# A transformer block pair on one core: first-half input projection and convolution made inside the expert stage, pooling on GpSimd, mask rows in attention

## The chip, the cores and the metric

The kernel runs on one core of a Trainium2 chip, in float32 throughout. The metric is the device time of one execution in microseconds (us), lower is better. The core has five instruction streams: TensorE (PE: matmuls; PEld: its weight loads), VectorE (DVE), ScalarE (ACT), GpSimd (POOL) and SyncE (SP, which here only issues weight loads). They share an on-chip memory (SBUF), 128 partitions wide; matmuls write into PSUM banks. Every dependence between engines is a semaphore wait written by hand, so an engine stands still at a wait even where later instructions could run.

## The reference

```python
def first_block(x, ...):
    h = rms_norm(x, g_mix[l]);  p = h @ w_in[l]
    y_a = mla_group(p[..., :MLA_COLS], ...)          # 8 heads, chunk-causal attention
    y_b = rwkv7_group(p[..., MLA_COLS:], ...)        # recurrent branch
    x = x + jnp.concatenate([y_a, y_b], -1) @ w_o[l]
    x = x + peer_ffn(rms_norm(x, g_ffn[l]), ...)     # 128 experts per token, rows gathered
    return x

def peer_ffn(...):   # per token: 8 heads x top 16
    u = expert_u[idx]; act = gelu(einsum('thkd,td->thk', u, hb)); vv = expert_v[idx]
    return einsum('thk,thkd->td', gate * act, vv)

def second_block(x, c, ...):
    h = layer_norm(x) * (1.0 + sc1) + sh1
    proj = h @ w_in[l]                               # 3584 columns
    a_val, a_gate, u_pool, gate_a, gate_b = split(proj)
    ya = a_val * sigmoid(a_gate)
    ya = causal_dwconv(ya, w_dw_a[l], b_dw_a[l])     # 31 taps, 512 channels
    ya = silu(layer_norm(ya, ...)) @ w_pw_a[l]
    yb = einsum(causal_multiscale_pool(u_pool), w_pool[l]) * pool_scale[l]   # windows 2, 4, 8, 16
    merged = sigmoid(gate_a) * ya + sigmoid(gate_b) * yb
    x = layer_norm(ALPHA * x + g1 * (merged @ w_out[l]), ...)
    ...                                              # gated FFN with 3 taps, 2 x 2816 columns
    return x
```

There are 512 tokens, 1024 channels; a query in a 64-token chunk sees that chunk and all before it.

## The kernel before

The 512 tokens are four tiles of 128 (`NT` = 4, t = 0 to 3; "tiles one and two" are t = 0, 1, tokens 0 to 255). The stages run one after another: the first block's projections, attention (32 units: tile x head), the recurrent branch, the output projection, the expert stage, and then the second block: input projection, convolution and pooling, `w_out`, the FFN.

**Channels.** PE hands results to ACT over four PSUM banks "a" (PA) and to DVE over four banks "d" (PD). Results are numbered; the table `JOBS` gives the first number of each stage on either channel, and ACT or DVE takes them strictly in order. A bank is reused once result j-3 was taken.

**Weights.** SP loads weight chunks of mostly 2048 KB in one fixed order into slots (mostly the three slots of `WR`). A load waits until the last use of the chunk that held the slot (L484), and all later loads wait behind it.

**Attention.** In unit u PE writes a score tile (L590), adds the mask to its last 128 columns by a second matmul of one row (L592: `lowrow` times `negrow`), transposes the probabilities of unit u-1 and multiplies those of u-2 with the values. Between units stand eight of the fourteen projections of the recurrent branch (`projection(m)`, eight matmuls of 512 columns each; `PR_EARLY` = 4 are made before, in front of the transposes of q and k). ACT copies each into `RAW`, and DVE mixes it with its token before (`mix(m)`, L1416 and L1417).

**Expert stage.** For each tile 128 steps k. POOL gathers one expert row per token, 1 MB for 128 tokens, into one of eight ring buffers (L1981), DVE forms the dot product (L1838), ACT makes the gate and a diagonal matrix of it (L1202, L1204, L1208), PE adds diagonal times row into two banks (L882) and so frees the buffer for the gather eight steps on. In tile t DVE also selects the experts of tile t+1. In tile 0 PE makes query projections between the steps (L859, 128 matmuls of 256 columns, ACT copies each result of eight).

**Second block's input projection.** Behind the last step, PE makes 28 blocks of 128 columns (seven chunks of `w_in2`, eight matmuls a block, all 512 tokens), the first four in two parts (L902, then L908 for the last tile). Chunk order: gate of the convolution, its value (the one that goes to DVE), pooling input, gates a, gates b. DVE multiplies value by gate (L1854), convolves 4 x 31 taps over 512 tokens (L1858, L1860), normalizes by two column sums that PE makes with a matrix of ones (4 matmuls each, placed in the last chunk), and then pools (L1894 to L1905). PE follows with the pooling product and the pointwise product (`yb`, `pw`), DVE merges (L1910 to L1916), then `w_out`.

## Time and profile before

| | |
|---|---|
| median of three runs | 2820.36 us (2818.66 to 2823.57) |
| the profiled execution | 2828.96 us, of which its span 2827.4 us |
| mean granted TensorE clock | 0.963 of full speed |
| PE busy | 2412.7 us (85%) |
| DVE busy | 1522.6 us (54%) |
| ACT busy | 704.7 us (25%) |
| POOL busy | 537.1 us (19%) |
| gathers by POOL | 512, 536.90 MB |

Times in the views count from the span's start. A float32 matmul is recorded twice on PE, so x64 there is 32 matmuls. A row's second number is busy time from the first start to the last end; for what one of several back-to-back instructions costs, take the distance of starts. "[7.29 <-issue]" is idle time ahead of the row and what ended it.

### The profile page before, as it was taken

To read this page: it belongs to the slowest core of one execution; us is meant where nothing else is said; L and a number is where in the kernel's file an instruction comes from. 1 tells how busy PE (TensorE), PEld (TensorE's weight loads), DVE (VectorE), ACT (ScalarE), POOL (GpSimd) and SP (SyncE) were. 2 spreads that over 40 slices of the span, in tenths; PEclk is the share of its full clock that TensorE was granted. 3 is DMA by queue.
4 is the path that set the end of the run, shared out by engine and by line. 5 is a ranking of instruction groups with operands and counts; after the bars stand their busy time and mean duration, and the time that the engine had idled before them with its cause. 6 is when DMAs were issued, how large, how long until landed. Compare 5 with 4: busy or idle time off the path is not lost.

```text
span 2827.4 us, 27190 instructions
## 1 busy us (share of the span) xinstructions
PE 2412.7 (85%) x9764; PEld 1184.4 (42%) x9764; DVE 1522.6 (54%) x3250; ACT 704.7 (25%) x2064; POOL 537.1 (19%) x516
## 2 busy tenths in 40 slices
PE   6889888798898977777777777788899898999998
PEld 3455478666444432222222222222354343444443
DVE  3555367638566646666576655554348464333204
ACT  1122221110333334333433343333200101111000
POOL 0000000000444534434343433333100000000000
PEclk9989869899999999999999999999999999999999
DMA  3301440311999999999999999999521312212110
GB/s 131 111 1 60 147 152 10 126 70 47 422 418 419 421 414 421 421 421 420 416 418 416 417 417 419 421 421 416 215 72 55 134 41 79 89 60 89 65 69 30
DMA packets 130102, 663.71 MB, mean 235 GB/s; under 512 B 9520, under 2 KB 12208, under 8 KB 64048
## 3 DMA queue, kind: packets, MB, share of 16 engines
q0 software_dynamic: 73728, 536.90, 45.8%
q1 hardware_dynamic: 56240, 125.08, 12.3%
q8 instruction: 77, 1.26, 0.2%
q14 instruction: 57, 0.47, 0.0%
HBM read 659.85 MB, written 2.10 MB: 234 GB/s over the span
## 4 chain that ended last, share of the span: by engine, by line
PE 53%; DMA 28%; DVE 8%; issue 6%; ACT 4%; PEld 1%; PEldq 0%; POOL 0%; SPq 0%; DVEq 0%; another core or an unknown queue 0%; ACTq 0%; POOLq 0%
DMA AR<-in_uv,C 27%; PE PA L525 22%; PE PD L882 10%; PE PD L525 8%; PE PA L859 2%; PE PD L954 1%; PE PA L954 1%; ACT C L1208 1%; PE PD L693 1%; PE PD L518 1%; PE PA L693 1%; DVE AR L1838 1%; ACT SC L1204 1%; PE PA L755 1%; PE PA L902 1%
## 5 line engine op out<-in xcount | busy, mean ns | idle before, releaser
L882 PE MATMUL PD<-AR,C 128*128 128x512 f32 x2048 | 1001.2, 614 | 262.2 <-ACT C L1208 261.2
L1838 DVE CUSTOM_DVE_ANT_0 AR<-AR,HN 128x1024 f32<-128x1024 f32 x512 | 626.3, 1224 | 509.9 <-DMA AR<-in_uv,C 506.9
L1981 POOL DMA_INDIRECT AR<-in_uv,C x512 | 536.9, 1049 | 1471.3 <-PE PD L882 740.8
L882 PEld LDWEIGHTS PD<-AR,C 128*128 128x128 f32 x2048 | 356.1, 190 | 842.1 <-ACT C L1208 567.9
L525 PE MATMUL PA<-AR,WR 128*128 128x512 f32 (+1 forms) x720 | 313.0, 603 | 4.7 <-ACT AR L1091 3.2
L1202 ACT ACTIVATE SC<-SC 128x1 f32<-128x1 f32 x512 | 103.7, 203 | 684.2 <-DVE SC L1838 683.8
L525 PE MATMUL PA<-HT,WR 128*128 128x512 f32 (+1 forms) x736 | 260.9, 515 | 0.0
L525 PEld LDWEIGHTS PA<-AR,WR 128*128 128x128 f32 (+1 forms) x720 | 138.1, 193 | 179.3 <-issue 176.4
L1208 ACT ACTIVATE C<-C,SC 128x128 f32<-128x128 f32 x512 | 205.5, 401 | 16.8
L525 PEld LDWEIGHTS PA<-HT,WR 128*128 128x128 f32 x736 | 125.6, 193 | 127.6 <-issue 127.6
L1204 ACT ACTIVATE SC<-SC,C 128x1 f32<-128x1 f32 x512 | 150.8, 294 | 16.6
L1949 DVE TENSOR_SCALAR HT<-HN,V 128x512 f32<-128x512 f32 x44 | 24.0, 546 | 197.1 <-ACT HN L1242 197.1
L525 PE MATMUL PD<-WR,HT 128*128 128x512 f32 (+1 forms) x320 | 120.0, 534 | 3.1 <-DVE HT L1916 1.6
L1242 ACT COPY HN<-PA 128x512 f32<-128x512 f32 x44 | 25.8, 586 | 267.8 <-PE PA L525 267.8
L1860 DVE SCALAR_TENSOR_TENSOR AR<-AR,V 128x512 f32<-128x512 f32 x120 | 90.2, 752 | 4.3
L954 PE MATMUL PD<-WR,AR 128*128 128x512 f32 x176 | 86.9, 610 | 5.3 <-DMA WR<-in_w_down 5.3
L954 PE MATMUL PA<-WR,AR 128*128 128x512 f32 x176 | 84.2, 593 | 1.4 <-ACT HN L1242 0.9
L525 PEld LDWEIGHTS PD<-WR,HT 128*128 128x128 f32 x320 | 57.0, 190 | 63.1 <-issue 58.8
L1014 ACT ACTIVATE SC<-SC 128x1 f32<-128x1 f32 (+4 forms) x33 | 6.8, 207 | 264.6 <-DVE SC L1278 261.3
L859 PE MATMUL PA<-HT,WR 128*128 128x256 f32 x256 | 72.1, 379 | 0.0
L859 PEld LDWEIGHTS PA<-HT,WR 128*128 128x128 f32 x256 | 48.9, 191 | 51.1 <-issue 49.8
L1960 DVE TENSOR_TENSOR HN<-PD,RW 128x512 f32<-128x512 f32 x4 | 2.8, 692 | 98.3 <-PE PD L954 98.3
(372 smaller groups left out, 2180.8 us busy)
## 6 DMA issues: line engine op xcount, KB each, us to landing
WR<-in_w_ada SPq DMA_DIRECT2D x12, 2048.0 KB, 9.5
WR<-in_w_in SPq DMA_DIRECT2D x11, 2048.0 KB, 7.9
WR<-in_w_up SPq DMA_DIRECT2D x11, 2048.0 KB, 7.9
WR<-in_w_down SPq DMA_DIRECT2D x5, 2048.0 KB, 7.9
WR<-in_w_pq SPq DMA_DIRECT2D x4, 2048.0 KB, 17.7
AR<-in_uv,C POOLq DMA_INDIRECT x512, 15.3
AR<-in_w_pq SPq DMA_DIRECT2D x3, 2048.0 KB, 12.9
WR<-in_w_o SPq DMA_DIRECT2D x2, 2048.0 KB, 8.3
```

The costliest lines, as they stand in the source:

```text
L518: ins = nc.tensor.transpose(b[0:cols, rows * i:rows * i + rows], src, ident[0:rows, 0:rows])
L525: ins = nc.tensor.matmul(b, lhsT, rhs, start=(i == 0), stop=(i == len(pairs) - 1))
L693: ins = nc.tensor.matmul(b[at:at + 64, 64 * i:64 * i + 64], lhsT, rhs, start=True, stop=True)
L859: ins = nc.tensor.matmul(b_pq[0][:, 0:2 * P], wq[:, k, P * (m % 4):P * (m % 4) + P], HT[:, k, 2 * P:S], start=(k == 0), stop=(k == KD - 1))
L882: ins = nc.tensor.matmul(acc[half], DG[:, j, :], UV[:, j, D + 512 * half:D + 512 * half + 512], start=(k == 0), stop=(k == NSEL - 1))
L954: ins = nc.tensor.matmul(banks[half][t], FT[:, k, P * t:P * t + P], w[:, kk, 512 * half:512 * half + 512], start=(k == 0), stop=(k == NF - 1))
L1202: tell(A(GEL[:, j:j + 1], DOT[:, j:j + 1], ACT.Gelu), "gelu")
L1204: tell(A(GEL[:, j:j + 1], GEL[:, j:j + 1], ACT.Copy, scale=GATE[:, t % 2, k:k + 1]), "gated")
L1208: tell(A(DG[:, j, :], ident, ACT.Copy, scale=GEL[:, j:j + 1]), "diag")
L1838: ttr(UV[:, j, 0:D], UV[:, j, 0:D], HN[:, t, :], 1.0, 0.0, ALU.mult, ALU.add, DOT[:, j:j + 1]).then_inc(s["dots"], 1)
L1860: link(stt(CV[:, m, :], YAP[:, m, j:j + 512], w[:, j:j + 1], CV[:, m, :], ALU.mult, ALU.add))
L1981: nc.gpsimd.indirect_dma_start(UV[:, ring_slot(turn), :], None, uv, bass.IndirectOffsetOnAxis(ap=IDX[:, t % 2, i:i + 1], axis=0),).then_in ...
```

## The change

It has four parts. (1) **Half in the expert stage.** All 28 blocks of the input projection are made for tokens 0 to 255 in the expert stage, one matmul of 256 columns a step, from step 32 of tile t = 2 on (96 steps there, 128 in t = 3); the chunks of `w_in2` are loaded once for it and a second time for tokens 256 to 511. ACT copies each block into free SBUF (with one Sigmoid for the gate after block 3). DVE multiplies value by gate at steps 100 to 103 of t = 2 and does the 124 taps of the first half, one a step, from step 112 on. The later input projection and convolution are then 256 tokens wide; ACT moves the parts made early to their places. (2) **Pooling** goes from DVE to GpSimd. (3) **Mask rows.** Four rows under q and k hold the mask, so the scores need one matmul; GpSimd writes them in 16 instructions as soon as the constants are there. (4) Two more projections of the recurrent branch stand ahead of the transposes of q and k (`PR_EARLY` = 6, three more `RAW` buffers), and two fewer between the units; DVE mixes two of them before unit 0.

```diff
+HALF_FROM, MUL_AT, CONV_FROM = 32, 100, 112
+def half_step_at(t, k):
+    if t == 2 and k >= HALF_FROM:
+        return k - HALF_FROM
+    return k + P - HALF_FROM if t == 3 else None
+def conv_step_at(t, k):
+    c = k - CONV_FROM if t == 2 else k + P - CONV_FROM if t == 3 else -1
+    return c if 0 <= c < 4 * CONV_K else None
...
-PR_EARLY, PR_IN_ATT = 4, 12
+PR_EARLY, PR_IN_ATT = 6, 12
...
-    put("lowrow", (j < 64) & (i == 0))
-    put("negrow", np.where((j >= 64) & (i == 0), np.float32(-1e30), np.float32(0)))
+    put("lowrow", j < 64)
+    put("negrow", np.where(j >= 64, np.float32(-1e30), np.float32(0)))
...
+        for q, i in enumerate(in2_order):
+            col_chunk(w_in2, 512 * i, 512, "a", half_job(4 * q + 3))
         for i, (ch, j) in zip(in2_order, in2_last):
             col_chunk(w_in2, 512 * i, 512, ch, (FIRST_A if ch == "a" else FIRST_D)["in2"] + j)
...
                 if i == CNUM["wout"]:
                     sp.wait_ge(s["row2free"], 1)
+                    sp.wait_ge(s["moved"], 4)
+                    sp.wait_ge(s["pooled"], 4)
                     sp.dma_start(R2, row2).then_inc(s["in_row2"], 16)
...
-                    nc.tensor.matmul(b[:, 0:nk], QKT[0:DQK, h, P * t:P * t + P], QKT[0:DQK, H + h, 0:nk],
-                                     start=True, stop=False)
-                    full("a", nc.tensor.matmul(b[:, nk - P:nk], cc("lowrow")[0:1, :], cc("negrow")[0:1, :],
-                                               start=False, stop=True))
+                    full("a", nc.tensor.matmul(b[:, 0:nk], QKT[0:DQK + NT, h, P * t:P * t + P],
+                                               QKT[0:DQK + NT, H + h, 0:nk], start=True, stop=True))
...
+            def half_step(c):
+                m, k = c // KD, c % KD
+                w = chunk(pe, CNUM["in2a"] + m // 4)
...
+                ins = nc.tensor.matmul(b_half[0][:, 0:2 * P], w[:, k, P * (m % 4):P * (m % 4) + P], HT[:, k, 0:2 * P],
+                                       start=(k == 0), stop=(k == KD - 1))
...
             for i in range(1, 7):
                 w = chunk(pe, CNUM["in2"] + i)
-                if i == 6:
-                    pe.wait_ge(s["conv"], 4)
-                    product("d", [(cc("ones"), CV[:, m, :]) for m in range(4)])
                 for m in range(4):
-                    if i == 6 and m == 2:
-                        pe.wait_ge(s["convsq"], 4)
-                        product("d", [(cc("ones"), HN[:, q, 0:512]) for q in range(4)])
+                    if i == 6 and m == 1:
+                        pe.wait_ge(s["conv"], 4)
+                        product("d", [(cc("ones"), CV[:, q, :]) for q in range(4)])
                     product("d" if i == 1 else "a",
-                            [(w[:, k, P * m:P * m + P], HT[:, k, :]) for k in range(KD)])
+                            [(w[:, k, P * m:P * m + P], HT[:, k, 2 * P:S]) for k in range(KD)], 2 * P)
+            pe.wait_ge(s["convsq"], 4)
+            product("d", [(cc("ones"), HN[:, q, 0:512]) for q in range(4)])
...
+                    c = half_step_at(t, k)
+                    if c is not None and c % KD == KD - 1:
+                        half_copy(c // KD)
...
+                    c = conv_step_at(t, k)
+                    if c is not None:
+                        j_, m = divmod(c, 4)
...
+                            ins = stt(CV1[:, m, :], YAP1[:, m, j_:j_ + 2 * P], w[:, j_:j_ + 1], CV1[:, m, :],
+                                      ALU.mult, ALU.add)
...
+            pool.wait_ge(s["in_const"], 64)
+            which = ident[DQK:DQK + NT, DQK:DQK + NT].unsqueeze(2).broadcast_to([NT, NT, P])
+            for g in range(2 * H):
+                row = cc("lowrow" if g < H else "negrow")[DQK:DQK + NT, :].unsqueeze(1).broadcast_to([NT, NT, P])
+                nc.gpsimd.tensor_tensor(QKT[DQK:DQK + NT, g, :].rearrange("p (t n) -> p t n", t=NT), which, row,
+                                        ALU.mult).then_inc(s["masked"], 1)
...
+            pool.wait_ge(s["a_free"], FIRST_A["in2"] + 8)
+            pool.wait_ge(s["d_free"], FIRST_D["in2"] + 4)
+            pool.wait_ge(s["moved"], 2)
+            pool.wait_ge(s["bufs"], 1)
+            for m, w in enumerate(POOL):
...
```

PE at the end of the expert stage, before: the last steps of two accumulating matmuls each (L882; x96 is 48 steps), the input projection (L902 to L525), with the two ones products (the x4 rows, which wait for DVE) inside its last blocks, then the pooling and pointwise products (x40) and `w_out`.

```order
L882 MATMUL PD<-AR,C 128x512 x96
L902 MATMUL PA<-HT,WR 128x384 x32
L518 MATMUL PD<-C,HN 128x128 x8
L908 MATMUL PA<-HT,WR 128x128 x32
L525 MATMUL PD<-HT,WR 128x512 x32
L525 MATMUL PA<-HT,WR 128x512 x128
L525 MATMUL PD<-AR,C 128x512 x4
L525 MATMUL PA<-HT,WR 128x512 x16
L525 MATMUL PD<-HN,C 128x512 x4
L525 MATMUL PA<-HT,WR 128x512 x16
L525 MATMUL PD<-AR,WR 128x512 x40
L525 MATMUL PD<-WR,HT 128x512 x32
```

PE at the same place after the change (L909 is the early half, L932 the step of the expert stage):

```order
L909 MATMUL PA<-HT,WR 128x256
L932 MATMUL PD<-AR,C 128x512 x2
L909 MATMUL PA<-HT,WR 128x256
L954 MATMUL PA<-HT,WR 128x128 x32
L554 MATMUL PD<-C,HN 128x128 x8
L960 MATMUL PA<-HT,WR 128x128 x32
L561 MATMUL PD<-HT,WR 128x256 x32
L561 MATMUL PA<-HT,WR 128x256 x136
L561 MATMUL PD<-AR,C 128x512 x4
L561 MATMUL PA<-HT,WR 128x256 x24
L561 MATMUL PD<-HN,C 128x512 x4
L561 MATMUL PD<-AR,WR 128x512 x40
```

A matmul of 256 columns now stands between the steps, the projection behind them has half the columns, the first ones product (`PD<-AR,C ... x4`) stands ahead of the last three blocks, and the second behind them.

GpSimd after the change; before it had the 512 gathers (the DMA row) alone. Rows up to the first windows of the pooling:

```order
L2048 TENSOR_TENSOR AR<-C 4x512 x16
L2061 DMA AR<-in_uv,C 128x2048 x512
L2086 TENSOR_TENSOR AR<-AR 128x512
L2091 TENSOR_TENSOR AR<-AR,C 128x16
L2092 TENSOR_SCALAR AR<-AR 128x496
L2093 TENSOR_TENSOR AR<-AR 128x512
L2085 MEMSET AR 128x16
L2086 TENSOR_TENSOR AR<-AR 128x512 x2
```

The 16 mask instructions stand at the front and the pooling at the end; L2086 to L2093 ahead of the MEMSET are the first of four windows, and each larger one has one addition (with a MEMSET) more.

PE at the start of attention, before (the first two rows are the last transposes of q and k, L590 and L592 scores and mask):

```order
L518 MATMUL PA<-C,AR 96x128 x4
L518 MATMUL PD<-C,AR 96x128 x4
L590 MATMUL PA<-AR 128x128
L592 MATMUL PA<-C 128x128
L590 MATMUL PA<-AR 128x128
L592 MATMUL PA<-C 128x128
L518 MATMUL PD<-C,AR 128x128
```

and after:

```order
L554 MATMUL PA<-C,AR 96x128 x4
L554 MATMUL PD<-C,AR 96x128 x4
L627 MATMUL PA<-AR 128x128 x2
L554 MATMUL PD<-C,AR 128x128
L627 MATMUL PA<-AR 128x128
L554 MATMUL PD<-C,AR 128x128
L561 MATMUL PD<-AR 128x64
```

One matmul a unit is gone.

## Rows read from the trace of the kernel before

**Rows 1.** The page: DMA's GB/s in 40 equal slices; median time to landing

```profile
GB/s 131 111 1 60 147 152 10 126 70 47 422 418 419 421 414 421 421 421 420 416 418 416 417 417 419 421 421 416 215 72 55 134 41 79 89 60 89 65 69 30
...
AR<-in_uv,C POOLq DMA_INDIRECT x512, 15.3
```

**Rows 2.** Windows: busy time of each engine, granted clock, DMA share, GB/s

```profile
713.00:2029.00 1316.00, 1057.11 (x2401) 418.00 (x2402) 800.87 (x1775) 496.43 (x1626) 529.22 (x504) 1.00 1.00 414
2029.00:2279.00 250.00, 238.83 (x617) 113.53 (x616) 142.54 (x215) 24.46 (x35) 0.00 (x0) 0.98 0.21 74
```

**Rows 3.** DMA queues in 980:1060, where three chunks of w_in2 land (packets, MB, share)

```profile
q1 hardware_dynamic: 3120, 6.29, 20.8%
```

**Rows 4.** Windows of the expert stage, tile 0, with query projections on PE

```profile
880.00:940.00 60.00, 54.58 (x153) 28.30 (x152) 40.90 (x91) 22.84 (x80) 27.40 (x23) 1.00 1.01 421
```

**Rows 5.** Timeline of PE, expert stage, tile 0 (start us, us)

```profile
906.27 1.88 PE L882 MATMUL PD<-AR,C 128*128 128x512 f32 x4
907.99 0.59 PE L859 MATMUL PA<-HT,WR 128*128 128x256 f32 x2
908.42 1.88 PE L882 MATMUL PD<-AR,C 128*128 128x512 f32 x4
```

**Rows 6.** Timeline of DVE and POOL, expert stage

```profile
1079.72 1.22 DVE L1838 CUSTOM_DVE_ANT_0 AR<-AR,HN 128x1024 f32<-128x1024 f32 x1 [1.25 <-DMA AR<-in_uv,C]
1079.82 1.94 POOL L1981 DMA_INDIRECT AR<-in_uv,C  x1 [2.08 <-PE PD L882]
1082.06 0.93 POOL L1981 DMA_INDIRECT AR<-in_uv,C  x1 [0.31 <-issue]
```

**Rows 7.** Timeline of PE from the expert stage's end to w_out

```profile
2028.62 20.88 PE L902 MATMUL PA<-HT,WR 128*128 128x384 f32 x64 [0.47 <-issue]
...
2052.67 9.04 PE L908 MATMUL PA<-HT,WR 128*128 128x128 f32 x64 [2.30 <-DVE HT L1845]
2061.55 27.63 PE L525 MATMUL PD<-HT,WR 128*128 128x512 f32 x64
...
2202.31 13.90 PE L525 MATMUL PA<-HT,WR 128*128 128x512 f32 x32
...
2240.66 36.54 PE L525 MATMUL PD<-AR,WR 128*128 128x512 f32 x80 [7.29 <-issue]
2278.78 27.73 PE L525 MATMUL PD<-WR,HT 128*128 128x512 f32 x64 [1.58 <-DVE HT L1916]
```

**Rows 8.** Timeline of DVE in the same stretch and at w_out

```profile
2163.56 23.59 DVE L1860 SCALAR_TENSOR_TENSOR AR<-AR,V 128x512 f32<-128x512 f32 x30
...
2219.68 0.69 DVE L1875 TENSOR_SCALAR HN<-PD 128x512 f32<-128x512 f32 x1 [12.15 <-PE PD L525]
...
2224.51 2.50 DVE L1880 TENSOR_TENSOR AR<-AR,HN 128x512 f32<-128x512 f32 x4
...
2245.55 5.04 DVE L1910 SCALAR_TENSOR_TENSOR HT<-PD,V,AR 128x512 f32<-128x512 f32 x6 [0.26 <-PE PD L525]
...
2340.26 1.28 DVE L1770 SCALAR_TENSOR_TENSOR X<-X,SC,AR 128x1024 f32<-128x1024 f32 x1
```

**Rows 9.** Timeline of PE, attention

```profile
150.21 1.09 PE L518 MATMUL PA<-C,AR 128*96 128x128 f32 x4 [18.11 <-DVE AR L1407]
...
237.79 0.48 PE L592 MATMUL PA<-C 1*128 1x128 f32 x2
238.20 0.55 PE L518 MATMUL PD<-C,AR 128*128 128x128 f32 x3
```

**Rows 10.** Timeline of DVE, start of attention

```profile
161.79 0.29 DVE L1429 TENSOR_REDUCE SC<-PA 128x1 f32<-128x128 f32 x1 [1.01 <-PE PA L592]
...
162.90 0.75 DVE L1417 SCALAR_TENSOR_TENSOR AR<-AR,V 128x512 f32<-128x512 f32 x1
```

**Rows 11.** Start: timeline of DVE, and time to landing of the last constant

```profile
14.26 0.16 DVE L1282 TENSOR_TENSOR SC<-SC 128x4 f32<-128x4 f32 x1
...
SC<-in_pos SPq DMA_DIRECT2D x1, 2.0 KB, 9.6
```

More of the change, by code:

```diff
@@ L254, in build @@
                  "topk", "idx", "dots", "geluv", "gates", "gelu", "gated", "diag", "uv_used", "csil", "rowdiag",
-                 "bufs", "conv", "convsq", "silu_in", "silu", "pooled", "merged",
+                 "bufs", "siga", "yam", "moved", "pooling", "conv", "convsq", "silu_in", "silu", "pooled", "merged",
                  "lnx", "upraw_used", "gelu_in", "ff", "fin", "row2free",
@@ L315, in build @@
         GF = C[:, CONST["lowrow"][0]:CONST["lowrow"][0] + D]
-        ROWDIAG = HN[:, 0:2, :].rearrange("p a b -> p (a b)")
+        ROWDIAG = CAND
+        YAP1 = ar(18432, 4 * 286, 4)
+        SGA1 = ar(19576, 1024, 4)
+        CV1 = SGA1
+        GA1 = ar(20600, 2048, 8)
+        UP1 = HN[:, 0, :].rearrange("p (a b) -> p a b", a=4)
+        GB1 = [HN[:, 1, :].rearrange("p (a b) -> p a b", a=4), HN[:, 2, :].rearrange("p (a b) -> p a b", a=4)]
         def y0(k):
@@ L862, in query_step @@
                     full("a", ins)
+            b_half = [None]
+            def half_step(c):
+                m, k = c // KD, c % KD
+                w = chunk(pe, CNUM["in2a"] + m // 4)
+                if c == 0:
+                    pe.wait_ge(s["a_free"], half_job(0))
+                if k == 0:
+                    b_half[0] = bank("a")
+                ins = nc.tensor.matmul(b_half[0][:, 0:2 * P], w[:, k, P * (m % 4):P * (m % 4) + P], HT[:, k, 0:2 * P],
+                                       start=(k == 0), stop=(k == KD - 1))
+                if k == KD - 1:
+                    full("a", ins)
             for j in range(16):
@@ L887, in _ @@
                         ins.then_inc(s["uv_used"], 1)
+                    if half_step_at(t, k) is not None:
+                        half_step(half_step_at(t, k))
                     if t == 0:
@@ L901, in _ @@
                 for k in range(KD):
-                    nc.tensor.matmul(first[m][:, 0:S - P], w[:, k, P * m:P * m + P], HT[:, k, 0:S - P],
+                    nc.tensor.matmul(first[m][:, 0:P], w[:, k, P * m:P * m + P], HT[:, k, 2 * P:3 * P],
                                      start=(k == 0), stop=(k == KD - 1))
@@ L907, in _ @@
                 for k in range(KD):
-                    ins = nc.tensor.matmul(first[m][:, S - P:S], w[:, k, P * m:P * m + P], HT[:, k, S - P:S],
+                    ins = nc.tensor.matmul(first[m][:, P:2 * P], w[:, k, P * m:P * m + P], HT[:, k, S - P:S],
                                            start=(k == 0), stop=(k == KD - 1))
@@ L1054, in _ @@
                 raw(t)
+            for m in range(NT, PR_EARLY):
+                raw(m)
             for g in range(0, 2 * H, 2):
@@ L1183, in turned_both, with half_copy @@
                     turned_block(HT, t, k0, lambda k: modc[:, 8 + k:9 + k], lambda k: modc[:, k:k + 1])
+            def half_copy(b):
+                q, m = divmod(b, 4)
+                dst = (SGA1[:, m, :], YAP1[:, m, 30:286], UP1[:, m, :], GA1[:, m, :], GA1[:, 4 + m, :],
+                       GB1[0][:, m, :], GB1[1][:, m, :])[q]
+                tell(nc.scalar.copy(dst, take()[:, 0:2 * P]), "a_free")
+                if b == 3:
+                    act.wait_ge(s["a_free"], half_job(3) + 1)
+                    tell(A(SGA1, SGA1, ACT.Sigmoid), "siga")
             gate_exp(0)
@@ L1418, in mix @@
                 tell(dve.nop(), "prt")
+            for m in range(2):
+                mix(m)
             units = [(t, h) for t in range(NT) for h in range(H)]
@@ L1442, in _ @@
                     link(ts(HN[:, t, 64 * h:64 * h + 64], b[:, 0:64], st_a[:, 32:33], None, ALU.mult), "d_free")
-                if u < PR_EARLY:
-                    mix(u)
+                if u + 2 < PR_EARLY:
+                    mix(u + 2)
                 if pr_after(u - 2) is not None:
@@ L1984, in _, with joined @@
                     ).then_inc(uv_full[ring_slot(turn)], 16)
+            def joined(ins, name="pooling"):
+                tell(ins, name)
+                pool.wait_ge(s[name], n[name])
+            tt_, ts_ = nc.gpsimd.tensor_tensor, nc.gpsimd.tensor_scalar
+            pool.wait_ge(s["a_free"], FIRST_A["in2"] + 8)
[3 more added lines that the diff above has]
+            for m, w in enumerate(POOL):
+                u = UP[:, m, :]
+                src = u
+                step = 1
+                bufs_ = [ar(16600, 528), ar(17128, 528)]
+                i = 0
+                while step < w:
+                    dst = bufs_[i % 2]
+                    if 2 * step < w:
+                        joined(nc.gpsimd.memset(dst[:, 0:16], 0.0))
+                    joined(tt_(dst[:, 16:528], src[:, 16:528], src[:, 16 - step:528 - step], ALU.add))
+                    src = dst
+                    step *= 2
+                    i += 1
+                cn_ = cc("cnt")[:, 16 * m:16 * m + 16]
+                joined(tt_(src[:, 16:32], src[:, 16:32], cn_, ALU.mult))
+                joined(ts_(src[:, 32:528], src[:, 32:528], 1.0 / w, None, ALU.mult))
+                joined(tt_(PO[:, m, :], src[:, 16:528], u[:, 16:528], ALU.subtract), "pooled")
 def kernel(**inputs):
```

101 lines of the change are left out of this document (55 added, 46 removed).

## The prediction

> **What bounds the kernel now.** I read the page first: from slice 11 to 28 DMA moves 414 to 422 GB/s [rows 1]. The table of windows says what that stretch is: over the 1316 us of the expert stage DMA is busy with share 1.00, while PE has 1057 us, DVE 801 and ACT 496 [rows 2]. So the gathers set the pace, about 2.49 us for each 1.048 MB at 421 GB/s, and every other engine has room; what is put into this stage is free on PE, DVE and ACT and costs full price on DMA. The 250 us behind it are the opposite: DMA share 0.21, PE busy 238.8 of 250 [rows 2], and the timeline of PE shows matmuls almost end to end from 2028.62 to the start of `w_out` at 2278.78, 250.2 us [rows 7]. In attention the timeline of PE has no idle entry in the units shown, but 18.11 us of idle before the transposes of q and k [rows 9].
>
> **End of the expert stage to `w_out`, the large gain.** I time it from E, 2028.62 [rows 7].
> - PE. The first four blocks are now twice 32 matmuls of 128 columns, 9.0 us each by L908; between them lie the transposes and DVE's eight small copies, which took from 2049.5 (2028.62 + 20.88) to 2052.67, 3.2 us [rows 7]. That is E+21.3. A matmul of 256 columns takes 0.43 us (907.99 to 908.42 [rows 5]), a block of eight 3.45; of 512 columns a block took 6.9 (27.63 for four [rows 7]). The four value blocks end at E+35.1, the sixteen next and one of the last chunk at E+94, where PE now waits for the convolution.
> - DVE. Its last multiplication ends at E+35.6. A tap on 512 columns takes 0.786 us (23.59 for 30 [rows 8]). 256 columns are in no row: such an instruction on 1024 columns takes 1.28 and on 512 it takes 0.75 [rows 8, 10], so 256 less columns save 0.265 and a tap is 0.52. Four rows of 30 taps and a cheaper first one are 16.0 each, 64.2 together: the convolution ends at C = E+100 if nothing disturbs DVE.
> - From C to `w_out`: ones product 3.5, three blocks 10.4, ones product 3.5, so C+17.4 (DVE's centring and squares, four instructions each like the 2.50 of L1880 [rows 8], hide in it). From there before's rows give the rest: 2219.68 to 2227.01, 7.3, for variance, root, reciprocal and scaling [rows 8]: C+24.7. Then `yb` leaves DVE every 0.84 us (5.04 for six [rows 8]); PE needs five of them gone before the pointwise product gets its first bank, 4.3, then eight products of 3.43, 27.4, and 1.6 for the merge [rows 7]: `w_out` starts at C+58. That is E+158, 92 us earlier than before.
> - Pooling on GpSimd. It starts when the pooling input of tiles three and four is copied, about E+50, right inside the convolution. Its 28 instructions (14 two-input ones of 512 columns, 4 of 496 with one input, 4 of 16, 6 memsets) have no row. DVE takes about 0.63 for such a two-input one (2.50 for the four of L1880), GpSimd's own gather instruction 0.93 to 1.94 [rows 6, 8]. I take 1.1, near the unhindered one, and 0.7 for one input: 19 us in all. GpSimd's own time is hidden: the result is due at C+17. Its neighbour is not: at 1079.82 a gather instruction began 0.10 us after a dot product of DVE and took 1.94 instead of 0.93, that is until the dot product's end and then its usual time [rows 6]. So a GpSimd instruction is kept out while DVE reads two SBUF tensors. Whether DVE is kept out in turn, no row shows: the price lies between nothing and GpSimd's whole 19 us. A tap reads two SBUF tensors, and I take the whole: C = E+119.
>
> The Trainium skill (SBUF — State Buffer, "SBUF: two separate sides") says that the port pair is an exclusive lock for a whole instruction between a GpSimd instruction and a DVE one with two SBUF inputs; by that rule the sum is the one with 19 us, without it the one of the rival below, and the row at 1079.82 agrees for one direction. The GPSIMD Engine Reference, section 3, gives 4497 ns for a two-input addition of 2048 columns, which makes an estimate of 1.1 us for 512.
>
> PE then idles from E+94 to E+119. Before, after 18.11 us of idle, four transposes took 1.09 us where later three take 0.55 [rows 9], about the ratio of TensorE's two levels, 1.2 and 2.4 GHz; a first ones product at the lower one costs 3.4 more. Together `w_out` starts at E+180.5: **-69.7 us**.
>
> **Loads, the price.** The seven chunks are loaded for the early half, and of the second set two more come before E; before, three came there (2048 KB each). Six more loads compete with the gathers: 12.6 MB at 421 GB/s are 29.9 us. By the share of DMA time it is more: 6.29 MB took 20.8% of 80 us, 5.5 a load [rows 3], 33.3 for six. I take **+32**. The step on PE grows from 1.72 to 2.15 us (906.27 to 908.42, where tile 0 had just this mix [rows 5]), below 2.49. ACT waits for PE in each block, some 2 us every eight steps; a gather takes 15.3 us from issue to landing where 2.5 is its share [rows 1], so this much delay empties nothing, and tile 0 had the same at 421 GB/s [rows 4]. DVE's tap adds 0.5 to 1.3 us. The later chunks load while PE works on two others, and the row vectors behind `pooled` have C-dependent work of 58 us in front: both free. If that cover went, a chunk costs its 8 to 10 us.
>
> **Attention.** Two projections of 6.9 us move into 18.11 us of idle [rows 9]: -13.8. 32 mask matmuls at 0.41 (237.79 to 238.20 [rows 9]): -13.1. Against it: DVE mixes two projections before unit 0, 1.4 each (0.75 and about as much [rows 10]), of which 1.01 was idle: +1.9. In the small units of tiles 0 and 1 PE may now wait for the exponentials, between 0 and the whole 0.41 of 16 units, 6.6; I take +3. With 14 us less idle ahead of the transposes the clock may stay at its upper level in them (1.09 for four now, against 0.55 for three later): 0 to 6 us, taken as -2. **-24**, from -19 to -29.
>
> **The start.** GpSimd's 16 mask instructions run from the landing of the constants (the last 9.6 us after its issue at about 4.1, so 13.7 [rows 11]), 17.6 us at 1.1. From 14.26 on DVE makes the rows that PE transposes and the angles; I count ten instructions with two SBUF inputs until 21.3, linked one by one, and PE's first projection waits for what follows them. By the same hold, ten times 1.1: **+11**, bounds 0 and 17.6.
>
> Sum: 11 - 24 + 32 - 69.7 = -50.7. The profiled execution (2828.96, span 2827.4 and 1.6 around it) would be 2778.3; it stood 8.6 above the median, so against 2820.36 I say **2769**.
>
> **Rivals.**
> 1. DVE is not held by GpSimd. Then start 0, C = E+100, PE idles 6 us only: -24 + 32 - 92 = -84, 2736. For it: no DVE row is stretched beside a gather. Against: those hold SBUF for a moment at most, and the hold in the other direction is visible. Chance 0.25.
> 2. GpSimd is slower than I think. At 1.94 us, the dearest of its rows, the pooling holds DVE 33 us instead of 19 and the start costs up to 19 instead of 11: 2769 + 14 + 8 = 2791; up to 2814 if its instructions take 3 us or `wout` loads then come late (they stand behind `pooled` on SP). Chance 0.16.
> 3. Slower than before: ACT's in-order wait for each early block isn't absorbed. ACT stands 2 to 2.7 us in each of 28 blocks; if the gathers felt it, 28 x 2.7 = 76 us, and 76 - 50.7 = +25, 2845. It turns slower at 1.9 us a block. Against it stands tile 0, with 16 such blocks at full GB/s [rows 4]. Chance 0.05.
> 4. The early half brings nothing because the end is bound elsewhere, and loads eat attention's gain: about 2815 to 2825. Against it are PE's 238.8 of 250 us. Chance 0.03.
> My forecast, 2755 to 2785, has 0.51.
>
> **How the numbers follow.** A measurement tells 0.2% (5.6 us) from no change. Rival 3 is slower, rival 4 mostly the same, the rest faster: 0.92, 0.03, 0.05. The range reaches from rival 1 with 6 us for the unknown clock and attention terms to rival 2's 2791 with 5: 2730 to 2796.
>
> **What would show it.** Right: expert stage about 32 us longer at 415 to 421 GB/s; convolution taps 0.49 busy, with some 19 us of gaps or stretched ones while GpSimd pools; PE idle before the first late ones product; `w_out` 180 us behind the last step; scores without L592's successor and an idle before the transposes of 4 us. Wrong: DVE rows of usual length beside GpSimd's (then 2736), a GpSimd instruction near 2 us, DMA share under 0.95 in t = 2 and 3, or the transposes of q and k starting late because ACT copies six projections.

## The result, and the profile after

The changed kernel takes 2774.74 us (median of 4 runs, 2770.58 to 2776.05) beside 2819.51 for the kernel before on the same chip (now the median of 4; with 3 it was 2820.36): ratio 0.9829, 95% interval 0.9813 to 0.9845, so 1.7% less, well clear of the noise. Its profiled span is 2768.5 us.

The kernel before was profiled a second time later (`e9_before_again`, span 2817.4, its time 2819.0 is nearer the median than that of the profile shown ahead). The stages, cut at PE's first product, the first transpose of q and k, the first product of the modulation, the load of `keys` just ahead of the first expert step, the first late projection (E) and `w_out`:

| stage | before | before again | after | forecast |
|---|---|---|---|---|
| start to first product | 24.7 | 24.8 | 36.0 | +11 |
| to the transposes of q and k | 125.6 | 125.6 | 127.1 | 0 |
| attention | 150.2 | 150.3 | 137.8 | -24 |
| modulation and recurrence | 411.2 | 398.7 | 393.9 | 0 |
| expert stage | 1316.9 | 1319.5 | 1354.9 | +32 |
| E to `w_out` | 250.2 | 250.1 | 170.6 | -69.7 |
| rest | 548.6 | 548.5 | 548.2 | 0 |

Against the second profile the sum is 48.9 us less. Every stage for which a change was forecast moved to that side, but three have another size than forecast: attention gave half, the end stage 10 more, and the first profile alone would credit 17 us to a stage that the change doesn't touch.

**Start.** DVE and GpSimd, timeline (start us, us; in brackets the idle time ahead and who ended it); this answers to [rows 11]:

```profile
14.11 0.52 DVE L1355 TENSOR_TENSOR SC<-SC 128x4 f32<-128x4 f32 x1
14.66 0.97 DVE L1356 SCALAR_TENSOR_TENSOR SC<-SC 128x4 f32<-128x4 f32 x1
...
16.67 5.84 DVE L1387 TENSOR_SCALAR HN<-X,SC 128x1024 f32<-128x1024 f32 x4
22.43 1.01 DVE L1403 CAST SC<-SC 128x4 f32<-128x4 int32 x1
...
29.53 0.94 DVE L1413 TENSOR_SCALAR SC<-SC 128x64 f32<-128x64 f32 x1
30.50 0.97 DVE L1414 TENSOR_SCALAR SC<-SC 128x64 f32<-128x64 f32 x1
31.50 0.19 DVE L1415 TENSOR_SCALAR SC<-SC 128x64 f32<-128x64 f32 x1
```

```profile
13.57 17.84 POOL L2048 TENSOR_TENSOR AR<-C 4x512 f32<-4x512 f32 x16 [13.14 <-DMA SC<-in_pos]
```

Look where the length of DVE's rows changes: from 22.43 on 0.94 to 1.02 us each until 31.50, 0.19 from there on, and GpSimd's row ends at 31.41. TENSOR_SCALAR and CAST, which have one tensor from SBUF, are held as long as those with two. PE's first product, behind 6.76 us of idle, then begins at the lower clock (0.50 granted in 36 to 38 us, where it was 1.00 before) and takes 29.13 us in place of 27.70; this is the 1.5 us of the second stage.

**Stages.** Windows of the changed kernel (busy time of each engine, granted clock, DMA share, GB/s), answering to [rows 2]:

```profile
163.10:300.90 137.80, 125.38 (x496) 78.03 (x496) 70.17 (x194) 35.94 (x112) 0.00 (x0) 0.87 0.09 31
300.90:694.80 393.90, 333.73 (x4617) 267.58 (x4616) 248.99 (x585) 75.63 (x153) 5.85 (x6) 0.90 0.28 101
694.80:2049.70 1354.90, 1136.73 (x2848) 511.04 (x2849) 851.75 (x1904) 507.50 (x1658) 558.02 (x506) 0.99 1.00 413
2049.70:2220.30 170.60, 143.62 (x616) 107.64 (x616) 107.93 (x187) 24.78 (x40) 25.41 (x28) 0.94 0.34 121
```

The expert stage still runs at DMA share 1.00 and 413 GB/s, with 80 us more of PE and 51 more of DVE inside. Attention has a granted clock of 0.87; before it was 0.95. PE's waits in attention (us in total, times, longest):

```profile
PE PD L554 <- ACT AR L1119: 8.8, 6, 4.7
PE PA L554 <- DVE AR L1481: 4.4, 1, 4.4
PE PD L554 <- DVE HN L1519: 2.3, 2, 1.7
PE PA L627 <- ACT AR L1109: 0.8, 1, 0.8
```

The idle of 18.11 us before the transposes [rows 9] is 4.4 now, as forecast; 12 us of waits inside the units stand beside it, where the kernel before had 4.7 (the window less PE's busy time).

**From E to `w_out`.** PE's timeline, answering to [rows 7]:

```profile
2081.32 58.87 PE L561 MATMUL PA<-HT,WR 128*128 128x256 f32 x272
...
2158.64 5.35 PE L561 MATMUL PD<-AR,C 128*128 128x512 f32 x8 [18.45 <-DVEq L1959]
2163.82 10.52 PE L561 MATMUL PA<-HT,WR 128*128 128x256 f32 x48
2174.18 3.60 PE L561 MATMUL PD<-HN,C 128*128 128x512 f32 x8
...
2220.30 27.73 PE L561 MATMUL PD<-WR,HT 128*128 128x512 f32 x64 [1.58 <-DVE HT L1990]
```

DVE's convolution beside it, answering to [rows 8], and some of GpSimd's pooling:

```profile
2082.06 0.41 DVE L1954 TENSOR_SCALAR AR<-AR,V 128x256 f32<-128x256 f32 x1
2082.51 16.46 DVE L1956 SCALAR_TENSOR_TENSOR AR<-AR,V 128x256 f32<-128x256 f32 x30
2099.14 1.38 DVE L1954 TENSOR_SCALAR AR<-AR,V 128x256 f32<-128x256 f32 x1 [0.18 <-DVE AR L1956]
2100.56 25.59 DVE L1956 SCALAR_TENSOR_TENSOR AR<-AR,V 128x256 f32<-128x256 f32 x30
2126.30 0.41 DVE L1954 TENSOR_SCALAR AR<-AR,V 128x256 f32<-128x256 f32 x1 [0.15 <-DVE AR L1956]
2126.75 15.59 DVE L1956 SCALAR_TENSOR_TENSOR AR<-AR,V 128x256 f32<-128x256 f32 x30
```

```profile
2095.80 1.11 POOL L2086 TENSOR_TENSOR AR<-AR 128x512 f32<-128x512 f32 x1 [66.64 <-ACT AR L1294]
...
2107.08 1.04 POOL L2086 TENSOR_TENSOR AR<-AR 128x512 f32<-128x512 f32 x1
...
2108.36 2.22 POOL L2086 TENSOR_TENSOR AR<-AR 128x512 f32<-128x512 f32 x2
2110.66 0.28 POOL L2091 TENSOR_TENSOR AR<-AR,C 128x16 f32<-128x16 f32 x1
2111.03 1.67 POOL L2092 TENSOR_SCALAR AR<-AR 128x496 f32<-128x496 f32 x1
...
2121.77 1.50 POOL L2093 TENSOR_TENSOR AR<-AR 128x512 f32<-128x512 f32 x1
```

GpSimd pools from 2095.80 to 2123.27. Thirty taps take 15.59 us without it, 25.59 beside it. The convolution is late for PE: 18.45 us of idle before the ones product. Single taps show that the hold comes and goes. The first of these begins beside a two-input addition of GpSimd (2107.08 above), the others beside its scaling of one input (2111.03):

```profile
2107.14 1.26 DVE L1956 SCALAR_TENSOR_TENSOR AR<-AR,V 128x256 f32<-128x256 f32 x1
...
2111.42 0.70 DVE L1956 SCALAR_TENSOR_TENSOR AR<-AR,V 128x256 f32<-128x256 f32 x1
...
2112.15 0.48 DVE L1956 SCALAR_TENSOR_TENSOR AR<-AR,V 128x256 f32<-128x256 f32 x1
```

The first tap ends at 2108.40, 0.28 us behind the addition's end at 2108.12; a tap alone takes 0.48. So it waited for the whole addition. This happens once for each of GpSimd's 14 two-input instructions of 512 columns: 13 taps take 1.14 to 1.38 us, and the TENSOR_SCALAR at 2099.14 takes 1.38 in place of 0.41, 11.0 us lost together. One tap beside each of the four scalings takes 0.70, 0.9 us lost together, and the taps between take their usual 0.48. In the other direction, GpSimd's two-input instructions take 1.04 us where no tap is in their way and up to 1.51 where one is under way.

### The profile page after: what moved, and what is told of

The parts are those of the page before. It is cut to its first block, busy times and chain, and to the rows that moved or that the text cites. A ratio compares the mean times of both kernels' runs of the same rounds, so it can differ in the third digit from the quotient of the medians.

```text
span 2768.5 us, 28188 instructions
## 1 busy us (share of the span) xinstructions
PE 2377.3 (86%) x10148; PEld 1260.4 (46%) x10148; DVE 1551.5 (56%) x3352; ACT 714.6 (26%) x2099; POOL 607.3 (22%) x560
## 4 chain that ended last, share of the span: by engine, by line
PE 48%; DMA 28%; DVE 12%; issue 6%; ACT 4%; PEld 1%; PEldq 0%; POOL 0%; SPq 0%; DVEq 0%; ACTq 0%
DMA AR<-in_uv,C 27%; PE PA L561 17%; PE PD L932 11%; PE PD L561 7%; DVE AR L1956 3%; PE PD L1005 1%; PE PA L894 1%; PE PA L1005 1%; DVE AR L1935 1%; ACT C L1271 1%; PE PD L554 1%; PE PD L728 1%; PE PA L728 1%; ACT SC L1267 1%; PE PA L554 1%
## 5 line engine op out<-in xcount | busy, mean ns | idle before, releaser
L932 PE MATMUL PD<-AR,C 128*128 128x512 f32 x2048 | 998.6, 612 | 214.7 <-ACT C L1271 210.6
L2061 POOL DMA_INDIRECT AR<-in_uv,C x512 | 563.9, 1101 | 1433.9 <-PE PD L932 750.2
L932 PEld LDWEIGHTS PD<-AR,C 128*128 128x128 f32 x2048 | 363.6, 191 | 675.0 <-ACT C L1271 402.7
L561 PE MATMUL PA<-HT,WR 128*128 128x256 f32 (+2 forms) x736 | 191.6, 422 | 0.0
L561 PEld LDWEIGHTS PA<-HT,WR 128*128 128x128 f32 x736 | 125.7, 192 | 60.3 <-issue 52.2
L909 PE MATMUL PA<-HT,WR 128*128 128x256 f32 x448 | 134.0, 381 | 2.9 <-ACT RW L1261 2.9
L909 PEld LDWEIGHTS PA<-HT,WR 128*128 128x128 f32 x448 | 85.6, 191 | 110.8 <-issue 110.8
L894 PE MATMUL PA<-HT,WR 128*128 128x256 f32 x256 | 72.6, 382 | 0.0
L894 PEld LDWEIGHTS PA<-HT,WR 128*128 128x128 f32 x256 | 49.1, 192 | 51.0 <-issue 49.7
L1956 DVE SCALAR_TENSOR_TENSOR AR<-AR,V 128x256 f32<-128x256 f32 x120 | 69.1, 576 | 4.3
## 6 DMA issues: line engine op xcount, KB each, us to landing
WR<-in_w_ada SPq DMA_DIRECT2D x12, 2048.0 KB, 11.3
```

Source lines behind the costliest of these rows:

```text
L561: ins = nc.tensor.matmul(b, lhsT, rhs, start=(i == 0), stop=(i == len(pairs) - 1))
L894: ins = nc.tensor.matmul(b_pq[0][:, 0:2 * P], wq[:, k, P * (m % 4):P * (m % 4) + P], HT[:, k, 2 * P:S], start=(k == 0), stop=(k == KD - 1))
L909: ins = nc.tensor.matmul(b_half[0][:, 0:2 * P], w[:, k, P * (m % 4):P * (m % 4) + P], HT[:, k, 0:2 * P], start=(k == 0), stop=(k == KD - 1))
L932: ins = nc.tensor.matmul(acc[half], DG[:, j, :], UV[:, j, D + 512 * half:D + 512 * half + 512], start=(k == 0), stop=(k == NSEL - 1))
L1956: link(stt(cv, YAP[:, m, 2 * P + j:S + j], w[:, j:j + 1], cv, ALU.mult, ALU.add))
L2061: nc.gpsimd.indirect_dma_start(UV[:, ring_slot(turn), :], None, uv, bass.IndirectOffsetOnAxis(ap=IDX[:, t % 2, i:i + 1], axis=0),).then_in ...
```

## The experiments

Every ratio is to the kernel before, timed beside it. The changed kernel has 0.9829 in its own comparison and 0.9819 in `e5_after_again`.

**e5_after_again and e10_after_third: the changed kernel again.**

> The changed kernel once more, as a control beside the three others of this call: 0.983 times the kernel before, about 2775.

2772.34 us, 0.9819 (0.9785 to 0.9853). The profile of e5 has the two stretches, attention and what follows, at other lengths than the first:

```profile
164.70:292.60 127.90, 115.35 (x496) 69.77 (x496) 69.58 (x195) 36.09 (x112) 0.00 (x0) 0.95 0.10 34
292.60:692.60 400.00, 338.15 (x4617) 269.01 (x4616) 248.97 (x585) 75.88 (x153) 6.80 (x7) 0.89 0.29 102
```

The same kernel, the same instructions (496 matmuls), 10 us less in attention at a clock of 0.95 where the first profile had 0.87.

> The changed kernel, profiled a third time, beside e9_before_again. Theory A: the same stretch takes 394 to 400 us, with 79 to 89 at the lower clock as in the first two profiles. Theory B: it can take 411 us too. Attention takes 128 or 138 us, according to 13 or 36 us at the lower clock.

Span 2771.8, one run of 2773.85 us; attention 137.8 at 0.87 and then 393.9 at 0.90, as in the first. This is what theory A says of the second stretch, but it doesn't refute B, which allowed 394 to 411; for the kernel before, the next run decides.

**e9_before_again: the kernel before again.**

> The kernel before, profiled a second time. Question: the stretch from the first product of the modulation to the load of the keys took 411.3 us before and 393.9 after, with 116 and 79 us of it at the lower clock, though the change touches nothing in it. Theory A (the clock's phases there belong to the kernel: how the work ahead of the stretch lies sets them): again about 411 us with 116 at the lower clock, and the time is 2820. Theory B (they vary from execution to execution, as attention did in the changed kernel, 137.8 and 127.9 us in two profiles): anywhere from 394 to 411 us, and the 17 us between the two first profiles are no part of what the change gives.

```profile
150.30:300.60 150.30, 145.60 (x592) 86.02 (x592) 69.76 (x195) 37.21 (x114) 0.00 (x0) 0.95 0.08 29
300.60:699.30 398.70, 336.93 (x4617) 270.00 (x4616) 248.80 (x585) 75.74 (x153) 5.78 (x6) 0.89 0.28 100
```

Theory B: 398.7 us this time, where the first profile took 411.2 at a clock of 0.86. So 12.5 of the 17 us lie between two profiles of one kernel and are no part of what the change gives. To compare such stretches I multiply the length by the granted clock, which gives about the length had PE, their bound, run at 2.4 GHz throughout (an estimate: the clock has two digits, so it is good to 1 us in attention and 2 in the other): 411.2 x 0.86 = 353.6 and 398.7 x 0.89 = 354.8 before, 393.9 x 0.90 = 354.5 and 400.0 x 0.89 = 356.0 after. Within that, the second stretch didn't change. Attention: 150.3 x 0.95 = 142.8 before, 137.8 x 0.87 = 119.9 and 127.9 x 0.95 = 121.5 after, some 22 less.

**e1_mask_late: the mask rows some 7 us later.**

```diff
             pool.wait_ge(s["in_const"], 64)
+            pool.wait_ge(s["sscan"], 2)
             which = ident[DQK:DQK + NT, DQK:DQK + NT]...
```

(`sscan` counts up when DVE's last two angle rows are done.)

> The changed kernel, with GpSimd's 16 mask instructions held back until DVE has made the angles of the rotary embedding (some 7 us later by the kernel before), so that they run while DVE reads PSUM. Theory (GpSimd holds every DVE instruction on SBUF beside it, also those with one input): DVE's small instructions take 0.19 us again where they took 0.97, HN's four scalings 2.7 us where they took 5.8, PE's first product starts 11 to 12 us sooner (24.7 us from the start of the span), and the time falls by 12 to about 2763. Rival 1 (something else is late, as the constants' landing): the start stays and the time is 2775. Rival 2 (the hold only moves): DVE's copies out of PSUM, 33 to 36 us in the changed kernel, are stretched in their turn and half of the gain is given back, 2769. A new phase of the granted clock behind the start can add or take up to 10 us in either case, so the start is judged by its rows.

2763.01 us, 0.9777 (0.9754 to 0.9800). DVE and GpSimd:

```profile
14.63 2.74 DVE L1387 TENSOR_SCALAR HN<-X,SC 128x1024 f32<-128x1024 f32 x4
...
19.21 0.20 DVE L1414 TENSOR_SCALAR SC<-SC 128x64 f32<-128x64 f32 x1
...
21.14 2.94 DVE L1377 TENSOR_SCALAR HT<-PD,V 128x512 f32<-128x512 f32 x4
```

```profile
21.25 16.07 POOL L2049 TENSOR_TENSOR AR<-C 4x512 f32<-4x512 f32 x16 [20.82 <-DVE SC L1420]
```

The first product starts at 24.2 in place of 36.0, the transposes at 149.6 in place of 163.1. Rivals 1 and 2 are out: DVE's four instructions that read PSUM take 0.75 us each beside GpSimd as without it (the 2.94 for all four, against 2.73 in the changed kernel, has a gap between the third and the fourth). GpSimd gains too, 1.00 us an instruction where it had 1.12. With the 1.5 us that PE's first product no longer loses, the transposes gain 13.5.

**e8_mask_one: GpSimd's instructions with one input, at the old place.**

```diff
-                nc.gpsimd.tensor_tensor(QKT[DQK:DQK + NT, g, :]..., which, row, ALU.mult)
+                nc.gpsimd.tensor_scalar(QKT[DQK:DQK + NT, g, :]..., which, 1.0, None, ALU.mult)
```

> The changed kernel, whose 16 GpSimd instructions at the start take one input from SBUF in place of two (they write only the pattern of the tiles and leave out the product with the mask's row, so the causal mask is missing from the scores), at the same place. Theory (the hold comes from GpSimd's reading two operands, as taps took 0.56 us beside GpSimd's one-input instructions and 0.81 to 0.93 beside those with two, against 0.49 alone): DVE's small instructions take 0.19 to 0.3 us each beside it, the first product starts at 24 to 26 us, and the time is 2763 to 2765, although each GpSimd instruction may take up to 1.7 us. Rival (any GpSimd instruction on SBUF holds DVE for its whole length): the small instructions take as long as GpSimd's, 1.0 to 1.7 us, the first product starts at 36 to 45 us, 2775 or more.

2767.50 us, 0.9795 (0.9773 to 0.9817):

```profile
14.73 3.95 DVE L1387 TENSOR_SCALAR HN<-X,SC 128x1024 f32<-128x1024 f32 x4
18.61 0.57 DVE L1403 CAST SC<-SC 128x4 f32<-128x4 int32 x1
...
20.48 0.22 DVE L1411 SCALAR_TENSOR_TENSOR SC<-SC 128x64 f32<-128x64 f32 x1
...
22.44 0.65 DVE L1416 TENSOR_SCALAR SC<-SC 128x64 f32<-128x64 f32 x1
```

```profile
13.61 25.96 POOL L2047 TENSOR_SCALAR AR<-C 4x512 f32<-4x512 f32 x16 [13.18 <-DMA SC<-in_pos]
```

GpSimd works longer (1.62 us each) and holds DVE less: the first product starts at 27.5, 8.5 us sooner than in the changed kernel and 2.8 later than before. The forecast was 24 to 26 us and 2763 to 2765. The theory holds for the most part, not wholly: DVE's instructions with two SBUF inputs are free (0.22), those with one (TENSOR_SCALAR, CAST, COPY) are held in part of the cases, 0.48 to 0.65. Of the 4.5 us over e1, 3.3 are the start. The edit changes the kind of instruction (TENSOR_TENSOR to TENSOR_SCALAR) together with the number of inputs, and no run tells the two apart; where this text says "two inputs" or "one input" of GpSimd, it means these two kinds. The 0.81 to 0.93 that the expectation names are means over held and free taps; a held one takes 1.14 to 1.38.

The Trainium skill (SBUF — State Buffer, "SBUF: two separate sides") also counts DVE's instructions with one input from SBUF in a two-port mode among those that contend for the pair; the rows of the changed kernel agree (TENSOR_SCALAR 0.94 to 0.97), though no row says which mode they ran in, and the prediction had left that half of the rule out. It says further that an instruction with two SBUF inputs is held by any GpSimd instruction that reads SBUF; the 0.22 here and the taps of 0.48 and 0.70 us beside GpSimd's scaling don't agree, and the measurement decides.

**e2_mask_old: the mask as before, by a second matmul.**

```diff
-                    full("a", nc.tensor.matmul(b[:, 0:nk], QKT[0:DQK + NT, h, ...], ..., start=True, stop=True))
+                    nc.tensor.matmul(b[:, 0:nk], QKT[0:DQK, h, ...], ..., start=True, stop=False)
+                    full("a", nc.tensor.matmul(b[:, nk - P:nk], cc("lowrow")[0:1, :], cc("negrow")[0:1, :], ...))
```

(and no mask instructions on GpSimd).

> The changed kernel with the mask made as before: a second matmul for each of the 32 units, and nothing on GpSimd at the start; all else stays. Theory: start 12 us sooner, attention 13 us longer (32 x 0.41), so 2775, no difference to the changed kernel beyond the clock's phases: the mask rows as they were placed bring nothing. Rival (in attention DVE and ACT are the bound once the projections are gone from between the units, and the second matmul is hidden): 2763.

2767.70 us, 0.9790 (0.9766 to 0.9814). The start is back at 24.0. Attention has

```profile
151.90:291.70 139.80, 132.35 (x560) 79.80 (x560) 69.58 (x194) 35.96 (x112) 0.00 (x0) 0.93 0.09 31
```

139.8 x 0.93 = 130.0, 9 above the changed kernel's 119.9 to 121.5, for 13.1 us of matmuls. The rest is PE's waits: 7.5 us in this window (139.80 less 132.35), 12.4 in the changed kernel's. So the mask rows bring 9 us in attention and cost 11 to 12 at the start: as placed, a little less than nothing. The time, 2767.70, lies between the theory's 2775 and the rival's 2763 and doesn't decide; the profile puts the rival out, though about a third of the matmuls' time was hidden.

**e7_pr4: the attention's order as before.**

```diff
-PR_EARLY, PR_IN_ATT = 6, 12
+PR_EARLY, PR_IN_ATT = 4, 12
```

(with the two entries of `JOBS` as before).

> The changed kernel with the attention's order as before: four projections of the recurrent branch ahead of the transposes of q and k, ten behind; mask rows, early half and pooling stay. Theory (two projections filled an idle of 18 us for 13.8): PE waits 18 us before the transposes where it waited 4.4, the stretch from the transposes to the first product of the modulation does not get longer by more than the 13.8 that the two projections take, and the time rises by 12 to 14 us, 2788. Rival (PE waits inside the units for ACT and DVE, 8.8 and 2.3 us, because projections are missing there, so that two more fill these waits): +3 to +5 us, 2779.

2780.98 us, 0.9847 (0.9823 to 0.9871): 9 us over e5, timed beside it. PE waits again,

```profile
163.39 1.09 PE L554 MATMUL PA<-C,AR 128*96 128x128 f32 x4 [18.14 <-DVE AR L1481]
```

and attention has

```profile
163.40:303.60 140.20, 129.65 (x531) 76.65 (x531) 69.69 (x194) 37.25 (x114) 0.00 (x0) 0.94 0.09 31
```

140.2 x 0.94 = 131.8, at an equal clock 11 us more than with the new order: near the forecast's 11.9 (13.8 less 1.9), and far from the rival's 3 to 5. The time alone, 9 us over e5, lies between the theory's 12 to 14 and the rival's 3 to 5. PE's waits for ACT inside the units stay (8.6 us of 8.8), so it isn't the missing projections that cause them; those for DVE fall from 2.3 to 0.6. In e2, with the mask matmuls back, PE waits 5 us less than in the changed kernel.

**e3_no_loads: the early half without its loads.** The early half's matmuls take the identity as weights; its values are not the reference's.

```diff
-        for q, i in enumerate(in2_order):
-            col_chunk(w_in2, 512 * i, 512, "a", half_job(4 * q + 3))
...
-                ins = nc.tensor.matmul(b_half[0][:, 0:2 * P], w[:, k, P * (m % 4):P * (m % 4) + P], ...
+                ins = nc.tensor.matmul(b_half[0][:, 0:2 * P], ident, ...
```

> The changed kernel without the early half's seven loads: its matmuls take the identity as weights, so the early half's values are not those of the reference, while the matmuls, ACT's copies and DVE's taps in the expert stage stay as they are. Theory (the gathers' stage is bound by DMA, and loads cost their share of it): the expert stage takes 1310 us as before the change where it took 1347, and the time is 2775 - 37 = 2738. Rival (some of the 37 is PE, ACT or DVE being late in tiles three and four, and the loads cost only their bytes at 421 GB/s, 30 us): 2745, and the stage stays 7 us over that of before. Rival 2 (the loads are hidden and the work is the price): 2775.

2737.10 us, 0.9680 (0.9648 to 0.9712). The expert stage:

```profile
692.80:2012.70 1319.90, 1123.57 (x2848) 512.51 (x2848) 851.38 (x1904) 505.98 (x1658) 575.55 (x505) 0.99 1.00 414
```

1319.9 us: no more than the kernel before in its second profile (1319.5), with all the early work in it. The same stage took 1351.0 to 1354.9 in the nine other profiles that have the loads, so they cost 31 to 35, and the work nothing that these profiles can tell (3.0 at most, against the first profile of before). The time fell by 35 us against e5 and by 38 against the changed kernel's first comparison, which meets the theory's 2738; the profile of e5, whose attention and recurrence are as long as here, has 33.0 us more in this stage. So the 37 of the theory is a little high by the stage. The rival's 30 us for the bytes is near, but its other 7 us, for work that is late, are not there.

**e4_pool_gap: pooling on DVE, where DVE waits.** GpSimd's block goes; DVE gets the same instructions in two parts:

```diff
                 tell(dve.nop(), "conv")
+            pool_part(0, 2)
             b = take()
...
                 tell(tt(HN[:, m, 0:512], CV[:, m, :], CV[:, m, :], ALU.mult), "convsq")
+            pool_part(2, 4)
             b = take()
```

> The changed kernel with pooling on DVE again, 28 linked instructions, in two parts, put where DVE waited in the changed kernel: two groups behind the convolution (5.5 us idle for PE's ones product) and two behind the squares (8.8 us idle). Theory: the 120 taps take 0.49 us each again, 62 us for the four channels where the changed kernel needed 76 from 2082 on, 12 us less; pooling takes 14.0 us in gaps of 14.3, but the first part, some 5 us, and the second, some 9, do not fit exactly, 1 to 2 us given back: 2764. Rival 1 (pooling lies on the chain after all, as PE's product of it stands ahead of the pointwise product): 14 us in place of the 12, 2775. Rival 2 (GpSimd's hold only filled time in which the taps waited anyway): 2789.

2759.82 us, 0.9756 (0.9722 to 0.9791), 4 us under the forecast; its four executions lie between 2751.7 and 2765.5. The start is as in the changed kernel (36.05). PE's timeline:

```profile
2052.65 7.38 PE L954 MATMUL PA<-HT,WR 128*128 128x128 f32 x64 [0.55 <-ACT HN L1243]
...
2151.37 5.94 PE L561 MATMUL PD<-AR,C 128*128 128x512 f32 x8 [6.60 <-DVEq L1983]
...
2213.70 8.85 PE L561 MATMUL PD<-WR,HT 128*128 128x512 f32 x20 [1.58 <-DVE HT L2016]
```

DVE's first thirty taps, which nothing holds:

```profile
2087.08 15.59 DVE L1980 SCALAR_TENSOR_TENSOR AR<-AR,V 128x256 f32<-128x256 f32 x30
```

The ones product starts at E+98.7 (108.9 in the changed kernel) behind 6.60 us of idle (18.45), and E to `w_out` takes 161.1 us; with pooling on GpSimd it took 170.6 to 174.3 in eight profiles. Pooling's 28 instructions take DVE 5.1 us in the first part and 8.5 in the second, and `w_out` still comes 62.3 us behind the ones product (61.7): they vanish in the waits. Rivals 1 and 2 are out.

This compares two new places for the pooling. What the move to GpSimd brought over the old place, no run shows. There DVE's pooling stood in the chain, from

```profile
2226.93 0.69 DVE L1894 TENSOR_TENSOR HN<-AR 128x512 f32<-128x512 f32 x1
...
2239.87 0.69 DVE L1905 TENSOR_TENSOR AR<-HN,AR 128x512 f32<-128x512 f32 x1
```

13.6 us in all, against 11.8 that GpSimd's costs by its hold: by this estimate the move gained about 2 us of the 80.

**e6_best: both repairs.**

> Both repairs together: the mask rows held back as in e1_mask_late, and pooling on DVE in the gaps as in e4_pool_gap. Theory (two holds at different places, each on the path that sets the end): the gains add, 12.5 us at the start and 9.6 at the end stage, so 22 us below the changed kernel, 2753. Rival (the clock's phases decide: less waiting early gives more time at the lower clock later): one of the two is lost, 2763 to 2765.

2746.90 us, 0.9730 (0.9710 to 0.9749), against 0.9819 for the changed kernel timed beside it (e5): 25 us less. First product at 24.9, E to `w_out` 160.2. The gains add, and this version beats both kernels.

## Why the prediction was right, step by step

The forecast of 2769 missed 2774.7 by 6 us; sizes were off in both directions.

- **Start, +11: right in size, partly by luck.** Measured +11.3, and e1 takes it all back. I counted ten DVE instructions with two SBUF inputs at 1.1 us. In fact only seven of them ran beside GpSimd, and nine with one input were held as well, which the forecast left out. These sixteen lost about 0.75 us each (5.0 us the seven, 3.9 the five small ones with one input, 3.1 the four row scalings), 12.0 in all: a wrong count times a wrong price gave nearly the right sum.
- **GpSimd's instructions, 1.1 and 0.7: the first near, the second mis-sized.** A two-input one on 512 columns takes 1.00 us at the start and 1.04 in the pooling where no tap is in its way; the one of 496 columns with one input takes 1.67, more than one with two. Pooling took 25.4 us, not 19.
- **The hold on the convolution, 19: right in kind, mis-sized.** "I take the whole" was the step that failed. From the first tap row to the ones product it is 76.5 us (2082.06 to 2158.6) against 64.7 in e4 (2086.63 to 2151.3): 11.8 us. The 14 two-input instructions, 15.4 of the 19, hold one DVE instruction each until they end, but a held tap then needs only 0.28 us more and not its 0.48, and a tap that is under way when the addition begins isn't held. So 0.8 us each is lost, 11.0 in all, and not 1.1 each. The scalings, 2.8 of the 19, cost 0.9, and the small instructions nothing that can be seen.
- **The convolution unhindered, E+100: right.** E+98.7 in e4 and E+97.1 in e6; a tap is 0.52 as worked out. PE's first blocks were mis-sized: two parts at 9.0 each by L908, where the changed kernel's took 7.4, so that the first taps start at E+32.4, 3 us sooner than forecast (in e4 one part took 9.0). C to `w_out`, 58 and 3.4 for the clock: 61.7 measured, but here two misses cancel, as the slower ones product cost 1.7 us and the rest took 60. So -79.6 in place of -69.7: 7 us of the difference are the hold, 3 the first blocks.
- **The row behind the 3.4.** 1.09 us for four transposes against 0.55 for three is a ratio of 1.5, not the 2 of the two levels; a row's length includes the last one's tail. By the distance of starts four of them take 0.85 to 0.9 us at the lower clock and 0.44 at the upper, and this is the ratio of 2.
- **Loads, +32: right.** 31 to 35 by e3; the stage grew by 38.0 over the first profile of before and by 35.4 over the second.
- **The early work hidden under the gathers (rival 3's opposite): right.** e3 has all of it and the old length.
- **Attention, -24: right at the same clock, -12.4 by the profile.** At 2.4 GHz it would be 22 less (142.8 to 119.9 and 121.5), of which e7 gives 11 to the order (forecast 11.9) and e2 9 to the mask (forecast 13.1 less 3 for waits; PE's waits grew by 5, from e2's 7.5 us to 12.4). What failed is "the clock may stay at its upper level", taken as -2: the transposes still begin at 1.09 us for four, and in two of three profiles of the changed kernel a stretch of attention ran at the lower clock and took 10 us back; the third profile has 127.9 us, -22.
- **The recurrence, no term: right, but only by the second profile.** The clock's phases there move by 12.5 us between two profiles of the same kernel.

Rival 1 (no hold) is refuted by the rows at the start, rival 2 (GpSimd slower) came half true in its own time without its effect, since the slow instructions are those that hold least. Rival 3 (ACT's waits reach the gathers) is refuted by e3, rival 4 (the end is bound elsewhere) by the 79.6 us that the end stage gave.

What stays open: what decides whether the lower clock falls into attention or into the modulation. It differs between executions of one kernel, but perhaps not by chance alone. Of the eight profiles that have both the new order and the mask rows, six show attention at 0.85 to 0.88 (137.5 to 141.5 us) and two at 0.95 (127.9 and 128.1); the four with the old order or the mask matmuls (before twice, e7, e2) show 0.93 to 0.95. The change may itself make the lower clock in attention more likely, as PE waits more there (12.4 us against 4.7, 10.6 and 7.5). No experiment here tests that.

## What to carry to other kernels

Work moved to GpSimd isn't free for DVE: here each two-input instruction on GpSimd held one SBUF instruction of DVE until it ended, those with one input included, while DVE's four reads of PSUM went on. Put it where DVE reads PSUM or waits (e1, 12 us for one line), or leave it on DVE in DVE's own waits (e4, 10 us). In a stage that is bound by DMA, work that fits into the other engines' idle time can be free and its bytes are not: here 28 blocks of matmuls and 124 taps cost nothing that the profiles show, their seven loads 31 to 35 us, against 80 us saved (some 2 of them by the pooling's move) where PE was the bound. And profile a kernel twice before giving 10 us of a PE-bound stretch to a change; the length times the granted clock was the steadier number here.
